# Ten matmuls with unused results among the decays' rows and the compression's narrow products of the second mixer

## The reference

```python
# fox: attention with decays; c is the running sum of log-sigmoids of a gate, per head
logf = jax.nn.log_sigmoid((f_logit + f_bias).astype(jnp.float32))
c = lax.cumsum(logf, axis=1).transpose(0, 2, 1)
s = q @ k.T * scale + (ci[..., :, None] - c[..., None, :])
# nsa: keys and values compressed over blocks of 32 tokens, one every 16: 15 blocks
blocks = kx[:, idx] + pos
hid = jax.nn.gelu(jnp.einsum('bnld,ldm->bnm', blocks, w1))   # 32 x 64 inputs, 128 outputs
return hid @ w2
# rg_lru: gates from block-diagonal products of the convolved input
r = jax.nn.sigmoid(jnp.einsum('bshi,hij->bshj', xb, w_gates[0]) + b_gates[0])
```

## Time and profile before

| | |
|---|---|
| median of 3 runs | 867.61 us (866.95 to 872.02) |
| the profiled execution's own time | 869.24 us |
| its span in the profile | 867.4 us |
| TensorE matmul busy | 817.1 us, 94% |
| VectorE busy | 548.1 us, 63% |
| ScalarE busy | 450.4 us, 52% |
| TensorE's share of the chain that ended last | 79% |

### The profile page before, as it was taken

How to read it: one execution, slowest core, us unless ns; L and a number is a source line. 1 busy time by engine, 2 the same in 40 slices (tenths; PEclk the granted TensorE clock), 3 DMA queues, 4 the chain that set the end, 5 groups by cost and what they waited for, 6 DMA issues and landing times.

```text
span 867.4 us, 14523 instructions
## 1 busy us (share of the span) xinstructions
PE 817.1 (94%) x5302; PEld 733.8 (85%) x5302; DVE 548.1 (63%) x1016; ACT 450.4 (52%) x849; POOL 62.9 (7%) x94
## 2 busy tenths in 40 slices
PE   3979997999899999999999999979889999999998
PEld 2679996889699889999999998958788899999997
DVE  3775434978759686666666675447766766666663
ACT  3455445565563565545454556066644654545552
POOL 7001002000034500000000020000000000000000
PEclk9579998999989799999999899569879999999999
DMA  8789864878639646666657475403205466565731
GB/s 266 248 223 299 262 184 137 246 220 249 209 115 297 188 140 198 195 179 185 191 172 196 97 188 159 128 28 95 74 26 169 131 185 190 173 196 173 203 105 49
DMA packets 194349, 151.07 MB, mean 174 GB/s; under 512 B 13298, under 2 KB 178600, under 8 KB 194176
## 3 DMA queue, kind: packets, MB, share of 16 engines
q1 hardware_dynamic: 188896, 143.61, 56.9%
q10 hardware_dynamic: 3760, 5.87, 1.8%
q0 software_dynamic: 1648, 1.00, 0.6%
HBM read 146.78 MB, written 3.41 MB: 173 GB/s over the span
## 4 chain that ended last, share of the span: by engine, by line
PE 79%; DVE 11%; ACT 5%; DMA 2%; issue 2%; ACTq 0%; DVEq 0%
PE ps L1833 19%; PE ps L1530 13%; PE ps L1531 12%; PE ps L1532 12%; PE ps L1835 10%; DVE w_lo L1018 3%; PE ps L1910 2%; ACT w_hi L657 1%; DMA arena<-in_x 1%; PE ps L1646 1%; PE ps L1768 1%; DVE sq L1101 1%; PE ps L1578 1%; PE ps L1746 1%; DVE sq L1075 1%
## 5 line engine op out<-in xcount | busy, mean ns | idle before, releaser
L1018 DVE TENSOR_TENSOR w_lo<-raw,w_hi 128x1024 fp32r<-128x1024 f32 (+3 forms) x223 | 270.7, 1233 | 104.8 <-ACT w_hi L657 104.5
L1833 PE MATMUL ps<-h,w_hi 128*128 128x512 f32 x704 | 254.0, 400 | 1.3 <-DVE h L1097 1.0
L657 ACT ACTIVATE w_hi<-raw 128x1024 fp32r<-128x1024 f32 (+3 forms) x223 | 227.0, 1038 | 30.8 <-PE ps L1532 9.1
L1835 PE MATMUL ps<-h,w_lo 128*128 128x256 f32 x704 | 199.3, 283 | 0.0
L1833 PEld LDWEIGHTS ps<-h,w_hi 128*128 128x128 f32 x704 | 133.1, 189 | 34.3 <-issue 1.7
L1530 PE MATMUL ps<-h,w_hi 128*128 128x256 f32 (+1 forms) x472 | 140.9, 299 | 6.4 <-DVE h L1097 2.2
L1531 PE MATMUL ps<-h,w_hi 128*128 128x256 f32 (+1 forms) x472 | 136.0, 288 | 0.0
L1532 PE MATMUL ps<-h,w_lo 128*128 128x256 f32 (+1 forms) x472 | 135.9, 288 | 0.0
L1835 PEld LDWEIGHTS ps<-h,w_lo 128*128 128x128 f32 x704 | 133.2, 189 | 0.1
L1530 PEld LDWEIGHTS ps<-h,w_hi 128*128 128x128 f32 (+1 forms) x472 | 92.9, 197 | 12.9 <-issue 10.1
L1530 PE MATMUL ps<-g_hi,w_hi 128*128 128x256 f32 x352 | 98.6, 280 | 0.0
(11 more groups left out here) (325 smaller groups left out, 1177.2 us busy)
## 6 DMA issues: line engine op xcount, KB each, us to landing
raw<-in_w_in SPq DMA_DIRECT2D x53, 512.0 KB, 5.1
raw<-in_w_ada SPq DMA_DIRECT2D x48, 512.0 KB, 4.6
raw<-in_w_down SPq DMA_DIRECT2D x44, 512.0 KB, 4.2
raw<-in_w_gate_up SPq DMA_DIRECT2D x44, 512.0 KB, 4.0
raw<-in_w_gate SPq DMA_DIRECT2D x22, 512.0 KB, 3.9
raw<-in_w_up SPq DMA_DIRECT2D x22, 512.0 KB, 5.0
raw<-in_w_o SPq DMA_DIRECT2D x8, 512.0 KB, 4.8
raw<-in_w_out SPq DMA_DIRECT2D x8, 512.0 KB, 3.6
```

What stands on the lines that cost most here:

```text
L657: A(w_hi[:, m % HL, 0:w], raw[:, n % RAW, 0:w], ACT.Copy).then_inc(hi_done, 1)
L1018: V.tensor_tensor(w_lo[:, m % HL, 0:w], raw[:, n % RAW, 0:w], w_hi[:, m % HL, 0:w].bitcast(f32), sub).then_inc(lo_done, 1)
L1833: T.matmul(bank[:, :], hi, h2[:, k, :, :].rearrange("p a b -> p (a b)"), start=(k == 0), stop=False, skip_group_check=True)
L1835: ins = T.matmul(bank[:, 0:SEQ], lo, h_hi[:, k, :], start=False, stop=(k == KC - 1), skip_group_check=True)
```

## The change

TensorE gets ten more matmuls of the helper, all into `ps[1]`: one ahead of the first and one ahead of the third of the decays' rows, and one ahead of each four of the compression's products. Each is two passes of 128 contraction rows and 256 columns. No other engine's program changes.

```diff
                 ins = T.matmul(ps[6][:, 304 + 4 * t:308 + 4 * t], cf[:, 2, t * P:(t + 1) * P], ident[0:FOX_HEADS, 0:FOX_HEADS],
                                start=True, stop=True)
             line(ins, "ccol_mm")
+            keep_awake(ps[1], 1)
             for h in range(FOX_HEADS):
+                if h == 2:
+                    keep_awake(ps[1], 1)
                 line(T.matmul(ps[2 + h // 2][:, SEQ * (h % 2):SEQ * (h % 2) + SEQ], selb[:, h, :], cf[:, 2, :],
                               start=True, stop=True), "crow_mm")
...
                     pe.wait_ge(raw_in[n % RAW], raw_count[n])
+                    keep_awake(ps[1], 1)
                     for k in range(8):
+                        if k == 4:
+                            keep_awake(ps[1], 1)
                         last = T.matmul(ps[7][:, 16 * kv:16 * kv + NCMP], raw[:, n % RAW, k * P:(k + 1) * P],
                                         xb[:, kv, 8 * half + k, :], start=(half == 0 and k == 0),
                                         stop=(half == 1 and k == 7))
```

## The result

The changed kernel takes 878.42 us (876.46 to 883.91, four runs), the kernel before 867.28 us (864.63 to 872.02): ratio 1.0136, 95% interval 1.0102 to 1.0170. It is slower by more than was forecast and just beyond the stated range.

A forecast was written before the change was run, and what follows sets the result against it. TensorE was taken to bound the kernel, its halved clock lengthening the path. The profiled 869.24 us plus 5.4 for the later compression gave 874.6; less the 1.63 offset, a median of about 873.0, range 863.0 to 877.5.

The forecast's parts named there:

- a group at half clock: One of the compression's eight groups, two wide and eight narrow passes: 2.58 us at half clock, 1.33 at full clock.
- 4.5 us of idle time as cover behind: TensorE's wait for VectorE's probabilities after the stretch, 4.6 us before, was to cover up to 3.8 us of slower work.
- n = 1.5: Compression: the clock falls in its second group, around 547 us; it ends at 563.7, 5.4 us later than before.
- 12 x 0.216 = 2.59: Decays' rows: eight old and four new passes at full clock take 2.59 us, so the compression starts 0.4 later.
- rival C: The clock falls among the decays' rows as now, added products failing their purpose: +8.3 us, 875.9; chance 0.15.
- offset of 1.63: Whole kernel: before's profiled execution, 869.24 us, was 1.63 above its median of 867.61; taken off the profile-based 874.6.
- a thin mixture and a still thinner start: Wide passes take only 0.43 of a group's 1.33 us, and thin decays' rows come first, so the clock falls early.
- 178.8 to 182.1: Existing rows nearest the new mixture: 27 passes, 16 of one column, clock half from 182.2; counted against holding.
- neither theory: The experiments' two: the mixture is too thin wherever it stands, or the thin decays' rows ahead lose the clock first.
- Rival A: The clock holds through the compression: 863.1 us, or 860.0 with factors and gates at full clock too; chance 0.18.
- the one-column products at 115.3: Existing products between dense chunks, 3.7 us with the clock full; counted as evidence that the clock would hold.
- 2.7 us: Compression: with all eight groups at full clock it ends at 555.6, 2.7 us earlier than before.

The follow-up runs named there:

- thick_start: The changed kernel with four added matmuls ahead of the first decays' row and three ahead of the third, instead of one each: 870.41 us, ratio 1.0056.
- after_again: The changed kernel unchanged, run again for more executions and a second profile: 876.39 us, ratio 1.0130 to the kernel before.
- comp_only: The changed kernel with only the eight added matmuls in the compression, none among the decays' rows: 873.09 us, ratio 1.0076 to the kernel before.
- swapped: The kernel before with the compression's operands exchanged, 15 columns as weights and 128x128 matrices streamed, no added matmuls: 857.48 us, ratio 0.9921.
- swapped_gates: As swapped, with the gates' four products between the factors instead of behind them; output not the reference's: 862.21 us, ratio 0.9951 to the kernel before.
- rows_only: The changed kernel with only the two added matmuls among the decays' rows, none in the compression: 869.51 us, ratio 1.0016 to the kernel before.
- narrow_added: The changed kernel with the ten added matmuls cut to 15 columns each: 872.36 us, ratio 1.0065 to the kernel before.
- comp_x2: The changed kernel with two added matmuls instead of one ahead of each four compression products: 868.66, 874.28, 882.21 and 884.34 us, no ratio.
- thick_both: The changed kernel with four and three added matmuls among the decays' rows and two ahead of each four compression products: 870.96 us, ratio 1.0068.
- rows_early: Against the kernel before: decays' transposes and rows ahead of the last chunk, eight added matmuls in the compression, none among the rows: 867.28 us, ratio 0.9995.

## Why the prediction was wrong

**The direction and the mechanism were right**: slower, because the clock falls at the compression's beginning and the added passes are then a cost at half clock. The forecast for the median was 873.0 us and 878.42 were measured. Of the 5.4 us between them 2.1 are mis-sized terms of the stretch, 0.8 lie outside it in the profiled execution, and 2.6 are the step from the profile to the median. The measured time lies 0.9 us above the range, so either of the two larger terms alone would have kept it inside. The prices held: a group at half clock 2.56 (forecast 2.58), at full clock 1.33 (thick_start), wide passes at full clock 0.216, factors and gates unchanged, no new wait, 4.5 us of idle time as cover behind.

**The terms that were mis-sized.** First, the point of the fall: I took n = 1.5 groups at full clock. The compression took 19.99 us, where all eight at half would be 20.5, so n = 0.4; that is 1.4 us. That the time was nearly hit ("around 547"; it was 547.6) is luck: this execution came to the stretch 1.1 us late, and in after_again the clock fell at 545.5. Second, the decays' rows: "12 x 0.216 = 2.59". They took 3.37, because where products of four contraction rows and the new ones meet, each of the four changes costs 0.2 (0.63 for two wide passes and 1.06 for four, not 0.43 and 0.86). Before, all eight stood in one row. That is 0.8 us. Together 7.5 instead of 5.4 in the stretch. What happened is nearly rival C's compression, all of it at half clock, but with the rows still at full clock, where C had the fall among them.

**The step that failed by most** was carrying the profiled execution's offset of 1.63 over to the changed kernel, as if it would lie above its median too; it lay 0.97 below. The profile of before was of a costly execution, and the changed kernel's of a cheap one: 2.9 us of the difference of the medians are not in the difference of the two profiles. I knew that before's runs spread over 5 us and still treated its profile as typical. It wasn't: of the four profiles in which the rows run where they stood, with nothing added among them, it is the only one that lost the clock in them; comp_only, swapped and swapped_gates ran all eight passes at full clock. Had before's clock lasted as long as comp_only's, 4.8 us from the first transpose instead of 2.0, the 2.8 us more at full clock would have saved about 1.4; this is an estimate from the two profiles. The rest, and how often each happens, stays open: there is one profile of before, and its executions also differ by microseconds ahead of the stretch.

**The reason given for the fall**, a thin mixture and a still thinner start, is neither refuted nor settled. These are the profiles with the rows where they stood; the time in the last column runs from the first transpose to the fall:

| profile | added among the rows, in the compression | first transpose | clock falls | us later |
|---|---|---|---|---|
| before | 0, 0 | 541.91 | 543.9 | 2.0 |
| rows_only | 2, 0 | 543.30 | 546.4 | 3.1 |
| comp_only | 0, 8 | 541.17 | 546.0 | 4.8 |
| changed kernel | 2, 8 | 543.01 | 547.6 | 4.6 |
| after_again | 2, 8 | 541.08 | 545.5 | 4.4 |
| narrow_added | 2, 8 of 15 columns | 538.87 | 543.7 | 4.8 |
| comp_x2 | 2, 16 | 546.32 | 565.4 | 19.1 |
| thick_start | 7, 8 | 539.13 | 557.0 | 17.9 |
| thick_both | 7, 16 | 538.21 | 560.2 | 22.0 |

thick_start and rows_early show that the mixture of one to four can hold the clock over all eight groups, which I had read 178.8 to 182.1 as speaking against. comp_x2 shows that with the changed kernel's own start a mixture of twice as many holds it too. So more wide work at either place goes with a clock that holds, and neither theory is right alone. The two added matmuls among the rows show no effect of their own: without them (comp_only) and with 15 columns (narrow_added) the clock fell as late as with them, and in rows_only, the same program as the changed kernel up to the compression, it fell 1.3 us sooner than in either profile of that. These are single executions; none of this says how often each happens. Rival A was nearer than I thought, since five more of the same matmuls went with 1.33 us a group in place of 2.56. Once lost, the clock didn't come back in the mixture in any profile (comp_only and both of the changed kernel).

One row that I counted for holding proves little: the one-column products at 115.3 took 3.63 us at full clock in before's profile, but 4.85 in the changed kernel's, at the same place and ahead of any change. A single execution's row shows that the clock can hold there, not that it does.

Even so, holding it doesn't pay: the profiled executions of thick_start and thick_both kept the clock through the compression, and the two kernels are 0.6% and 0.7% slower than before.

## What to carry to other kernels

Matmuls with unused results pay twice if they don't keep the clock: their own passes, and those at half speed. Before adding them, compute what is gained if the clock holds for all of the stretch (here 2.7 us by the prediction's estimate) against what is lost if it doesn't (7.5 measured); with such odds they need a margin, and here the margin cost as much as the clock gave. Look first whether the narrow work itself can be made wide by exchanging the operands: that cut the stretch from 16.4 to 9.5 us in its profile and won 0.8% (interval 0.5% to 1.1%). And take more than one profile of either kernel before carrying a profile's offset over to a median.

## What the runs showed of the hardware that I had not expected

The clock can be lost with TensorE 100% busy (before, 541.9 to 543.9, then 0.50), and whether it is kept is a matter of the single execution: the same eight passes of the rows lost it in the profile of before and kept it in those of comp_only, swapped and swapped_gates. A pass that streams 128 columns against 15 weights' columns takes 0.11 us at full clock (swapped), and one that streams 15 against 128 takes 0.10 (a row of eight in thick_start, 547.05 to 547.87), so at full clock it hardly matters which operand is the weights. Where products of four contraction rows and of 128 follow one another, each change of kind cost 0.2 us at full clock (0.63 for two wide passes in place of 0.43).
